# One-core decoder step: four moves in the order of decode scores, modulation blocks and softmax

## What is computed

```python
def layer(x, c, l, pos0, attention, ...):
    mod = jnp.dot(jax.nn.silu(c), w_ada[l]) + b_ada[l]          # 6 * 1024 values per conditioning row
    sh1, sc1, g1, sh2, sc2, g2 = [m[:, None, :] for m in jnp.split(mod, 6, axis=-1)]
    h = rmsnorm(x, norm1_g[l]) * (1.0 + sc1) + sh1
    proj = h @ w_in[l]
    u_pool, q, k, v, u_ssm = jnp.split(proj, cuts, axis=-1)
    y_a, pool_new = pool_mix(u_pool, ...)
    o = attention(q, k, v, lam, l)        # differential: two softmaxes per head, 4 heads
    y_b = (rmsnorm(o, subln_g[l]) * (1.0 - lam_init)).reshape(B, S, ATTN_WIDTH)
    y_c, h_re, h_im = ssm_mix(u_ssm, ...)
    mix = jnp.concatenate([y_a, y_b, y_c], axis=-1)
    x = x + g1 * (mix @ w_out[l])
    h2 = rmsnorm(x, norm2_g[l]) * (1.0 + sc2) + sh2
    x = x + g2 * moe_ffn(h2, ...)         # top-8 of 64 experts and a shared one
```

## Time and profile before

| | |
|---|---|
| median of 3 runs | 1879.39 us (1878.71 to 1882.89) |
| the profiled execution's own time | 1877.9 us |
| its span, first to last instruction | 1876.2 us |
| mean granted clock of TensorE | 0.942 |
| busy: TensorE, weight load | 1717.8 us (92%), 990.6 us (53%) |
| busy: VectorE, ScalarE, GpSimd | 663.6 us (35%), 353.3 us (19%), 693.9 us (37%) |
| DMA | 588.89 MB, mean 314 GB/s |

### The profile page before, as it was taken

The page is one execution under the profiler, slowest core; times in us unless marked ns, Lnnn a source line. Parts: engine busy times, 40 slices in busy tenths (PEclk is TensorE's granted clock), DMA queues, the critical chain, the costliest instruction groups (busy, mean ns, idle before and its releaser), DMA issues.

```text
span 1876.2 us, 28165 instructions
## 1 busy us (share of the span) xinstructions
PE 1717.8 (92%) x11215; PEld 990.6 (53%) x11215; DVE 663.6 (35%) x1666; ACT 353.3 (19%) x799; POOL 693.9 (37%) x754
## 2 busy tenths in 40 slices
PE   6898988899999999999588988988999999999964
PEld 3773565455555555555267446744555555555533
DVE  3876455212212321221479654621121221212125
ACT  3222331111113111111031233111111111111101
POOL 1215005345454545454012410344545454444420
PEclk9986999999999999999879799999999999999995
DMA  9448577998999999999934886699999999999943
GB/s 310 135 157 304 188 288 284 409 356 307 410 408 380 379 373 371 376 358 351 345 110 130 286 272 227 261 417 387 372 374 364 366 363 381 359 376 357 380 151 133
DMA packets 216639, 588.89 MB, mean 314 GB/s; under 512 B 67705, under 2 KB 147277, under 8 KB 162622
## 3 DMA queue, kind: packets, MB, share of 16 engines
q1 hardware_dynamic: 146224, 506.99, 71.1%
q0 software_dynamic: 67232, 79.73, 12.4%
q10 hardware_dynamic: 3054, 0.38, 0.2%
HBM read 775.22 MB, written 56.95 MB: 444 GB/s over the span
## 4 chain that ended last, share of the span: by engine, by line
PE 79%; DMA 9%; DVE 6%; SPq 2%; issue 2%; ACT 1%; POOL 1%; DVEq 0%; ACTq 0%; POOLq 0%
PE ps L1344 36%; PE ps L1357 16%; PE ps L906 8%; DMA xg<-hrows,idx_x 4%; PE ps L1061 4%; PE ps L1244 3%; DMA ypart<-yrows_k 2%; PE ps L949 2%; DMA wide<-in_w_ada 1%; SPq L621 1%; PE ps L1297 1%; PE ps L935 1%; PE ps L1327 1%; PE ps L957 1%; DMA raw<-in_w_ada 1%
## 5 line engine op out<-in xcount | busy, mean ns | idle before, releaser
L1344 PE MATMUL ps<-raw,xTs 128*64 128x256 f32 x6144 | 745.6, 394 | 1.7 <-ACT xTs L1611 1.4
L1344 PEld LDWEIGHTS ps<-raw,xTs 128*64 128x64 f32 x6144 | 418.9, 136 | 269.0 <-issue 37.9
L855 POOL DMA_INDIRECT yrows_k<-ytok,idx_y x192 | 195.7, 1020 | 514.2 <-DVE ytok L2030 470.5
L1357 PE MATMUL ps<-dn,scratch 128*64 128x512 f32 x1536 | 361.6, 592 | 1.5 <-DVE scratch L2034 1.5
L2024 DVE TENSOR_TENSOR scratch<-scratch,ps 128x128 f32<-128x128 f32 x192 | 55.2, 288 | 719.8 <-ACT scratch L1633 719.8
L848 POOL DMA_INDIRECT xg<-hrows,idx_x x192 | 198.1, 1032 | 110.6 <-issue 57.6
L2030 DVE COPY ytok<-ps 128x512 f32<-128x512 f32 x192 | 132.8, 692 | 213.6 <-PE ps L1357 213.6
L1611 ACT ACTIVATE xTs<-ps 128x512 f32<-128x512 f32 x192 | 114.6, 598 | 396.5 <-PE ps L906 396.5
L1357 PEld LDWEIGHTS ps<-dn,scratch 128*64 128x64 f32 x1536 | 107.9, 135 | 145.3 <-issue 110.6
L1633 ACT ACTIVATE scratch<-ps 128x128 f32<-128x128 f32 x192 | 53.3, 278 | 638.2 <-PE ps L1344 638.2
L906 PEld LDWEIGHTS ps<-cst,xg 128*128 128x128 f32 x768 | 81.3, 141 | 173.9 <-issue 146.1
(11 more groups left out here) (382 smaller groups left out, 1400.4 us busy)
## 6 DMA issues: line engine op xcount, KB each, us to landing
raw<-in_exp_w_gate SPq DMA_DIRECT2D x128, 1024.0 KB, 7.3
raw<-in_exp_w_up SPq DMA_DIRECT2D x128, 1024.0 KB, 9.8
dn<-in_exp_w_down SPq DMA_DIRECT2D x128, 1024.0 KB, 8.9
wide<-in_w_ada SPq DMA_DIRECT2D x32, 1024.0 KB, 8.3
wide<-in_w_in SPq DMA_DIRECT2D x16, 1024.0 KB, 8.5
ypart<-yrows_k SPq DMA_DIRECT2D x16, 1024.0 KB, 12.1
raw<-in_w_ada SPq DMA_DIRECT2D x14, 1024.0 KB, 12.5
narrow<-in_w_out SPq DMA_DIRECT2D x6, 1024.0 KB, 8.3
```

The source lines that it names most:

```text
L855: pool.indirect_dma_start(yrows_k.rearrange("t (h d) -> (t h) d", h=2), bass.IndirectOffsetOnAxis(ap=idx_y[:, b:b + 1], axis=0), ytok[n % ...
L1344: ins = mm(ps[64 * h:64 * h + 64, 2 + n % 2, 0:256], xTs[n % 2][:, k % 4, 64 * (k // 4):64 * (k // 4) + 64], w[:, k, h], start=k == 0, sto ...
L1357: ins = mm(ps[64 * h:64 * h + 64, 5 + n % 2, :], actT[:, n % 2, 64 * j:64 * j + 64], dn[n % NDOWN][:, j, 512 * h:512 * h + 512], start=j = ...
```

## The change

Four moves, on TensorE and in ScalarE's stream to match; no instruction is added or dropped.

1. The decode scores are turned right after block 5. Turn 4 comes behind scores(0).
2. Block 6 and turn 5 come behind the values of the first four requests, where block 7 was. The loop turns 6 to 9 and makes 7 to 10; turn 10 follows the loop.
3. Block 11 is made in the output projection behind parts 0 to 3, and turned behind part 5 (in bank 6); ScalarE copies between the squares.
4. scores(1) comes behind the decode weights (and waits until ScalarE has copied block 5 out of its bank); its exponents come ahead of the copies of blocks 5 and 6 on ScalarE.

```diff
@@ TensorE
             ada(layer, ADA_FIRST + 1, 1)
-            W(glu_gate)
-            ada_turn(layer, ADA_FIRST, 4, 256)
-            ada(layer, ADA_FIRST + 2, 7)
-            W(ada_late, 1)
-            ada_turn(layer, ADA_FIRST + 1, 4, 256)
             W(st_copied)
             pe.wait_ge(dec_scored.sem, dec_scored.by(layer, 1))
...
             scores(0)
-            W(ada_late, 2)
-            ada_turn(layer, ADA_FIRST + 2, 4, 256)
-
-            scores(1)
+            W(glu_gate)
+            ada_turn(layer, ADA_FIRST, 4, 256)
+
             W(comb_ready)
...
             mm(ps[0:NS, 7, 64:96], aps[:, :], comb[:, :], start=True, stop=True).then_inc(dec_weights.sem, 1)
+            pe.wait_ge(ada_copied.sem, ada_copied.by(layer, ADA_FIRST + 2))
+            scores(1)
             W(w32_ready)
...
             for b in range(4):
                 decode_values(b)
-            ada(layer, ADA_FIRST + 3, 7)
+            W(ada_late, 1)
+            ada_turn(layer, ADA_FIRST + 1, 4, 256)
+            ada(layer, ADA_FIRST + 2, 7)
...
-                    W(ada_late, 3 + h)
-                    ada_turn(layer, ADA_FIRST + 3 + h, 4, 256)
+                    W(ada_late, 2 + h)
+                    ada_turn(layer, ADA_FIRST + 2 + h, 4, 256)
...
-                    ada(layer, ADA_FIRST + 4 + h, 7)
+                    ada(layer, ADA_FIRST + 3 + h, 7)
                 else:
                     W(w_copied, n + 1)
-                    W(ada_late, 4 + h)
+                    W(ada_late, 3 + h)
...
             W(pv_copied, HEADS)
+            W(ada_late, 2 + HEADS)
+            ada_turn(layer, WIDE_ADA - 2, 4, 256)
             W(ada_late, 3 + HEADS)
-            ada_turn(layer, WIDE_ADA - 1, 4, 256)
-            W(ada_late, 4 + HEADS)
...
             for c in range(4):
                 out_part(c, out_order[4:]).then_inc(out_made.sem, 1)
+            ada(layer, WIDE_ADA - 1, 7)
             for c in range(4, KD):
...
                 out_part(c, out_order).then_inc(out_made.sem, 1)
+                if c == 5:
+                    ada_turn(layer, WIDE_ADA - 1, 6, 0)
@@ ScalarE
             ada_columns(ADA_FIRST, 4, 256)
-            ada_copy(layer, ADA_FIRST + 2, 7)
-            ada_columns(ADA_FIRST + 1, 4, 256)
 
             W(dec_max)
...
-            ada_columns(ADA_FIRST + 2, 4, 256)
             exps(0)
-            ada_copy(layer, ADA_FIRST + 3, 7)
+            exps(1)
+            ada_columns(ADA_FIRST + 1, 4, 256)
+            ada_copy(layer, ADA_FIRST + 2, 7)
...
-                if n + 1 < 2 * HEADS:
+                if n >= 1 and n + 1 < 2 * HEADS:
                     exps(n + 1)
                 if n % 2 == 0:
-                    ada_columns(ADA_FIRST + 3 + h, 4, 256)
+                    ada_columns(ADA_FIRST + 2 + h, 4, 256)
                 turned(n)
                 if n % 2 == 0:
-                    ada_copy(layer, ADA_FIRST + 4 + h, 7)
+                    ada_copy(layer, ADA_FIRST + 3 + h, 7)
...
-            ada_columns(WIDE_ADA - 1, 4, 256)
+            ada_columns(WIDE_ADA - 2, 4, 256)
...
-            square(out_added, squares_2, layer)
+            for k in range(KD):
+                W(out_added, k + 1)
+                act_(hT[:, k, :], xT[:, k, :], ACT.Square).then_inc(squares_2.sem, 1)
+                if k == 3:
+                    ada_copy(layer, WIDE_ADA - 1, 7)
+                elif k == 5:
+                    ada_columns(WIDE_ADA - 1, 6, 0)
```

## The result

The changed kernel took 1891.92 us (median of 18 runs, 1885.07 to 1900.24), the kernel before 1881.97 in the same comparison (18 runs, 1873.26 to 1898.17). The ratio is 1.0059, with a 95% interval of 1.0042 to 1.0075: 11 us slower (8 to 14), where 1.9 us faster had been forecast. The time is outside the predicted range and on the other side of no change.

The account below looks back on a forecast made before the run. TensorE was taken as the bound, four fifths of the chain that ended last. Gain 9.4 before the loop, less 5.5 for the projection and 2.0 for w_out, gave 1.9 us faster: 1877.5 from 1879.4, range 1873 to 1884.

Parts of the forecast that it names:

- The stretch: End of block 5 to scores(2): scores(2) 6.1 us earlier in layer 0, 3.3 in layer 1, together 9.4.
- the upper bound of 5.5: Block 5's turn and block 6 ahead of scores(2): 2.9 us at full clock, 5.5 at the low one; 3.5 taken.
- The table load holds the exponent: ScalarE before the loop: table load behind the column copy delays the decode exponent to 166.5, 1.8 us of new delay.
- rival D: Exponent waits for more than the load, by as much again: 2.8 us less gain, 1880.3; chance 0.02.
- The w_out wait: Ahead of the output projection: w_out's first piece lands late, 1.3 and 0.7 us of new wait, 2.0 paid.
- The next piece: Second piece of w_out in the projection: lands at 222.1, in time by 0.8 us.
- rival C: Larger w_out wait from shared DMA engines: 0.5 us more per layer, perhaps twice; 1878.5 to 1879.5; chance 0.06.
- The projection: Output projection gains block 11 and a turn: 2.75 us per layer, 5.5 paid.
- The loop: Softmax loop: same count and shapes of blocks, only the clock can change it; costed at nothing.
- Rival B: Clock stays low through block 5's turn and block 6; with layer 1's loop 4.8 us slower, 1884.2; chance 0.17.
- Layer 1's 30.9 us at 1.00: Softmax loop in the earlier trace: 30.9 us at clock 1.00 in layer 1, against 33.6 at 0.90 in layer 0.

Follow-up runs that it names:

- the second execution of before: Kernel before once more, unaltered; its stretch before the loop took 27.3 and 22.1 us, with waits for block 6's weights of 8.0 and 6.2 us.
- the filled kernels: Versions with useless matmuls added in TensorE's waits; the changed kernel with 8, 3, 2 and 2 of them: 0.9990 to the kernel before, 1878.36 us against 1880.94.

## Why the prediction was wrong, step by step

- **The stretch: right in its mechanism, its size with some luck.** Forecast 6.1 and 3.3 us of gain, 9.4; the stretches of the two first profiles differ by 4.2 and 4.6, 8.8, and over three executions by 10.5 (7.2 without the second execution of before). The waits of 3.4 and 2.0 us in the earlier trace rows were taken as the kernel's own, and over three executions they ranged from 0.7 to 8.0. The order within it came as written: the exponent started at 165.62 (forecast 166.5, and VectorE ended its scores 0.9 earlier), the values at 169.68 (170.6), scores(2) at 178.41 (177.5). What differs is block 5's turn and block 6, which took 1.88 + 3.41 at the low clock in layer 0, near the upper bound of 5.5 and not the 3.5 taken; from the turn's start to scores(2) it was 5.1 in layer 0 and 2.8 in layer 1, and 4.1 in the mean of three executions.
- **The table load holds the exponent: right.** It does so with no drain behind it: load 164.33 + 1.28 = 165.61, exponent at 165.62. The drain of some 1380 ns that the Trainium skill, "ScalarE: Activation LUTs", section What ACT_TABLE_LOAD costs, adds at a switch is not there, neither ahead of the load nor behind it (ScalarE's copy ends at 164.31), so rival D falls.
- **The w_out wait: right.** 1.3 and 0.7 forecast; 0.9 and 0.5, then 0.8 and 1.7, and 1.0 and 0.3. The next piece was in time, as written (no idle ahead of 224.71). Removing the wait altogether gave some 3 us, within the error, so rival C carried little.
- **The projection: mis-sized.** Block and turn cost 2.9 (2.75 forecast), but the same step took the projection's clock as 1.00, from the earlier trace rows. With the loop's end as it now is, the first 16 records run wholly or mostly at 1.2 GHz (5.4 to 6.2 us for 3.83): 1.4 us per layer more in the mean.
- **The loop: here the prediction failed.** The step was "same count, same shapes, so only the clock can change it ... I take nothing". Its premise held: the records, VectorE's and ScalarE's times are the same. The conclusion put the one thing that could change at zero. It changed by 10.5 us of low clock and, at 0.44, 4.6 us of time per layer, 9.3 in both. From the 1.9 us faster of the forecast to the 11 slower measured there are 13; the loop's clock is 9.3 of them and the projection's 2.8.
- **Rival B named the mechanism and missed its place and price.** It had the clock staying low through the two pieces behind the values, which is what happened in layer 0 (cost 2), and 2.7 in layer 1's loop. The price was bounded by the 2.7 us by which the loops in the earlier trace rows differed, as if the worst seen in one execution were the worst there is. The loop at the low clock for half its length, 38.9 us, lay outside any row of before. A bound from rows would have been at hand: the block at 3.64 against 1.92, twice the time for all that TensorE does in the 26.1 busy us of a loop at the full clock.
- **Layer 1's 30.9 us at 1.00 was read as the loop's length and was a draw.** Two further executions gave 34.2 and 33.6 for the same loop.

What the filled kernels show is that the changed kernel's low clock needs the idle time of TensorE in these places, since work that computes nothing takes it away. Idle time alone doesn't bring it. In five of the six loops of the changed kernel the clock fell in the turn right behind the loop's longest wait, of 1.23 or 1.24 us, as in the two lines at 193.53 and 194.92; but a loop in each of the three executions of the kernel before has the same wait (1.22 or 1.23) and the turn behind it at the full speed, 1.06. What isn't shown is why the changed kernel's loop, whose own waits are nearly those of before, mostly keeps the low clock for 17 us where the kernel before kept it for 9 or less. Filling the 3 us ahead of the values removes most of it, so the wait that the change put there has a part; but the kernel before waited 0.7 to 8.0 us for weights there, with no more low clock in the loop behind the longest wait (1.3). Its wait ended 17.6 us ahead of the loop (165.96 to 183.6), the changed kernel's 11.4 ahead (167.05 to 178.41). Over three executions the distances are 15.2 to 18.9 in the kernel before and 8.3 to 11.6 in the changed one, but within the changed kernel the low clock doesn't follow them (9.4 with 5.4 us of low clock, 8.4 with 19.0). Whether that distance decides was not tried. The Trainium skill, "TensorE: Matmul & The Clock Gate", section A second HAM failure mode: psum-queue depth-cycling, says that small idle gaps between groups of matmuls, often enough repeated, make the clock swing between its levels; the trace agrees as far as it goes, with four waits of 1.2 us at most in the loop and the fall in the midst of them.

## What to carry to other kernels

When a change removes work from TensorE's stream or moves a wait, don't cost the unchanged part behind it at its old length: price it also with half of it at 1.2 GHz, and look at more than one execution before taking a stretch's granted clock as its property. An idle microsecond is not only lost, it can be followed by some 17 at half the clock, as here; a block of real work that can stand in such a gap is worth more there than in a stretch that is full anyway, and a few useless matmuls in the gap are a cheap test of whether the clock is what costs. Taking work from a place with gaps (the loop) to a full one (the projection) was paid in full there, and here saved nothing, since the clock of the loop fell. And a wait for a DMA is a draw as well: don't count the one of a single profile as won.

## What the runs showed of the hardware

- 28 useless matmuls per layer made the changed kernel 13 us faster (8 to 18), at a mean granted clock of 0.9504 instead of 0.9351.
- The same instruction stream came with loops of 33.8 to 39.8 us in three executions. Most of the spread between runs of the kernel before goes with the clock: over its 27, 29, 35 and 16 runs in the four comparisons the mean granted clock explains 67 to 73% of the variance of the time, with 0.35 to 0.50 us for a microsecond of low clock. With filling the spread of single runs was smaller too (standard deviation 2.3 us over 12 runs against 4.2 over 18).
- The wait for block 6's weights took 0.7 to 8.0 us in three executions of the same kernel, by layer.
- Low clock costs less than its share: 0.44 us per microsecond in the loop, 0.47 in the projection, against 0.50 if everything in it took twice the time. The rest are waits for other engines, which stay as they are.
